# Two edits in a two-layer hybrid diffusion block: gate inputs fetched back in five transfers, and 32 instead of 64 streamed columns in the RWKV doubling levels

## The reference: what is computed

```python
def rwkv_scan(s0, r, w, k, v, kk, a, reverse, emit):
    ...
        sa = jnp.einsum('bhvk,bhk->bhv', s, kk_t)
        s = (s * w_t[:, :, None, :] - sa[..., None] * (kk_t * a_t)[:, :, None, :]
             + v_t[..., None] * k_t[:, :, None, :])
...
def merge_branches(h, ys, w_branch, w_gate, b_gate, w_o):
    gates = jax.nn.sigmoid(h @ w_gate + b_gate)
    acc = gates[..., :D_MODEL] * (ys[0] @ w_branch[0])
    for i in range(1, N_BRANCH):
        acc = acc + gates[..., i * D_MODEL:(i + 1) * D_MODEL] * (ys[i] @ w_branch[i])
    return acc @ w_o
```

## Time and profile before

| | |
|---|---|
| median of 3 runs | 1743.99 us (1742.7 to 1755.26) |
| the profiled execution: its own time | 1740.77 us |
| the profiled execution: span of the trace | 1739.0 us |
| PE busy, weight loads busy | 93%, 76% of the span |
| DVE, ACT, POOL busy | 53%, 45%, 17% |
| mean granted clock of TensorE | 0.973 of 2.4 GHz |
| RWKV passes: forward and reverse of layer 0 | about 347 to 416 and 416 to 491 us |
| RWKV passes: forward and reverse of layer 1 | about 1280 to 1342 and 1342 to 1409 us |

### The profile page before, as it was taken

The page is one execution under the profiler, slowest core; times in us unless marked ns, Lnnn a source line. Parts: engine busy times, 40 slices in busy tenths (PEclk is TensorE's granted clock), DMA queues, the critical chain, the costliest instruction groups (busy, mean ns, idle before and its releaser), DMA issues.

```text
span 1739.0 us, 33048 instructions
## 1 busy us (share of the span) xinstructions
PE 1611.8 (93%) x14136; PEld 1321.1 (76%) x14136; DVE 913.3 (53%) x1438; ACT 783.1 (45%) x1285; POOL 302.3 (17%) x241
## 2 busy tenths in 40 slices
PE   5899999988899998899999998999988889989997
PEld 3678767776666676688888885887776679879997
DVE  3154445476334444555555224565786446567754
ACT  4232355473342233544444223624766453566653
POOL 0041033513010000011112000121452110012201
PEclk8899999999899999999999999999999999989999
DMA  9473345504682222132222534734523284436553
GB/s 324 107 190 98 112 159 176 176 7 148 185 301 73 96 73 73 49 97 97 97 97 62 124 100 148 222 124 134 168 66 124 55 278 155 145 98 194 182 164 116
DMA packets 230496, 234.49 MB, mean 135 GB/s; under 512 B 5904, under 2 KB 217232, under 8 KB 230224
## 3 DMA queue, kind: packets, MB, share of 16 engines
q1 hardware_dynamic: 210720, 190.17, 34.6%
q0 software_dynamic: 15024, 35.92, 7.6%
q10 hardware_dynamic: 4608, 6.29, 1.1%
HBM read 216.63 MB, written 15.73 MB: 134 GB/s over the span
## 4 chain that ended last, share of the span: by engine, by line
PE 67%; DVE 5%; issue 3%; ACT 3%; DMA 0%; POOL 0%; ACTq 0%; DVEq 0%; POOLq 0%
PE ps L1878 16%; PE ps L1879 16%; PE ps L1880 16%; PE ps L2262 5%; PE ps L2120 2%; PE ps L2108 1%; PE ps L1921 1%; PE ps L2159 1%; DVE X L1392 1%; PE ps L2082 1%; PE ps L1901 1%; DVE wlo L1326 1%; PE ps L1902 1%; PE ps L1903 1%; PE ps L1859 1%
## 5 line engine op out<-in xcount | busy, mean ns | idle before, releaser
L899 ACT ACTIVATE whi<-ring 128x1024 fp32r<-128x1024 f32 (+1 forms) x264 | 275.3, 1046 | 550.7 <-PE ps L1880 493.1
L1326 DVE TENSOR_TENSOR wlo<-ring,whi 128x1024 fp32r<-128x1024 f32 (+1 forms) x264 | 326.5, 1242 | 218.5 <-ACT whi L899 217.8
L1878 PE MATMUL ps<-H,whi 128*128 128x512 f32 (+1 forms) x656 | 220.6, 336 | 2.2 <-DVE wlo L1326 2.2
L1880 PE MATMUL ps<-H,wlo 128*128 128x512 f32 (+1 forms) x656 | 220.4, 336 | 0.0
L1879 PE MATMUL ps<-H,whi 128*128 128x512 f32 (+1 forms) x656 | 220.4, 336 | 0.0
L1878 PE MATMUL ps<-HR,whi 128*128 128x512 f32 (+1 forms) x568 | 202.2, 356 | 2.2 <-DVE wlo L1326 1.8
L1880 PE MATMUL ps<-HR,wlo 128*128 128x512 f32 (+1 forms) x568 | 198.3, 349 | 0.0
L1879 PE MATMUL ps<-HR,whi 128*128 128x512 f32 (+1 forms) x568 | 198.1, 349 | 0.0
L1878 PEld LDWEIGHTS ps<-H,whi 128*128 128x128 f32 x656 | 124.5, 190 | 15.6 <-issue 2.8
L1880 PEld LDWEIGHTS ps<-H,wlo 128*128 128x128 f32 x656 | 124.5, 190 | 12.9
L1879 PEld LDWEIGHTS ps<-H,whi 128*128 128x128 f32 x656 | 124.5, 190 | 12.5
(11 more groups left out here) (318 smaller groups left out, 3064.2 us busy)
## 6 DMA issues: line engine op xcount, KB each, us to landing
ring<-in_ffn_up SPq DMA_DIRECT2D x44, 1024.0 KB, 5.1
ring<-in_ada_w SPq DMA_DIRECT2D x40, 1024.0 KB, 5.6
ring<-in_w_gate SPq DMA_DIRECT2D x32, 1024.0 KB, 6.1
ring<-in_w_in SPq DMA_DIRECT2D x24, 1024.0 KB, 7.2
ring<-in_ffn_down SPq DMA_DIRECT2D x32, 512.0 KB, 4.0
ada<-in_ada_w SPq DMA_DIRECT2D x8, 1024.0 KB, 11.9
WB<-in_w_branch POOLq DMA_DIRECT2D x8, 1024.0 KB, 7.5
ring<-in_w_o SPq DMA_DIRECT2D x8, 1024.0 KB, 5.2
```

Source lines behind the costliest of these rows:

```text
L899: act.activation(whi[half_slot(m)][:, 0:kn, :], ring[:, SLOT[raw] % RING, 0:kn, P * half:P * half + P], ACT.Copy).then_inc(hi_done, 1)
L1326: dve.tensor_tensor(wlo[half_slot(m)][:, 0:kn, :], ring[:, SLOT[raw] % RING, 0:kn, P * half:P * half + P], whi[half_slot(m)][:, 0:kn, :].b ...
L1878: pe.matmul(o[:, c0:c1], hi[:, i, :], part(0, k), start=(k == 0), stop=False)
L1880: last = pe.matmul(o[:, c0:c1], lo[:, i, :], part(0, k), start=False, stop=(k == kn - 1))
```

## The change

**Gate inputs.** A helper `hidden_back(part, k0, kn)` fetches `kn` of the 8 row blocks of one part. POOL issues part 1 whole, behind `receptance(1)` and ahead of `to_chunk_end(1)`, that is in the forward chunk loop. Part 0 stays at the old place and comes in four pieces of two row blocks, each issued only when everything before it has landed (`h_back` counts five transfers, and PE waits for all five).

**Levels.** The masks `m2` to `m32` are stored with their 32 non-zero columns alone. `sx` streams only the even blocks of TN's columns, `XS` holds 32 columns of each block, `sy` streams those 32, and TN is updated in its even blocks alone. The number of instructions of each engine but POOL stays the same; POOL issues six transfers more over both layers.

```diff
@@ constants @@
     for z in LEVELS:
-        put(f"m{z}", ((s // z) % 2 == 1) & (t // z == s // z - 1))
+        even = t[:, (t[0] // z) % 2 == 0]
+        put(f"m{z}", ((s // z) % 2 == 1) & (even // z == s // z - 1))
...
-        XS = at("XS", 88, [2, 2, NB, CH])
+        XS = at("XS", 88, [2, 2, NB, CH2])
...
+        def even_blocks(v, z):
+            if len(v.shape) == 2:
+                return v.rearrange("p (g two n) -> p g two n", two=2, n=z)[:, :, 0, :]
+            return v.rearrange("p b y (g two n) -> p b y g two n", two=2, n=z)[:, :, :, :, 0, :]
@@ POOL @@
+                def hidden_back(part, k0, kn):
+                    src = hsave[part, P * k0:P * (k0 + kn), c0:T].rearrange("(k p) t -> p k t", p=P)
+                    pool.dma_start(HG[:, part, k0:k0 + kn, c0:T], src).then_inc(h_back[l], 16)
...
                 receptance(1)
+                pool.wait_ge(h_saved[l], 32)
+                hidden_back(1, 0, KT)
                 to_chunk_end(1)
                 bonus(1)
-                pool.wait_ge(shift_done, 7 * (2 * l + 1) + 7)
                 pool.wait_ge(mm_done, done_at(("tok", l, 1, "k", 1)))
                 pool.wait_ge(bonus_done, 4 * l + 4)
                 pool.wait_ge(lg_done, l + 1)
-                pool.wait_ge(h_saved[l], 32)
-                for part in range(2):
-                    pool.dma_start(HG[:, part, :, c0:T], hsave[part, :, c0:T].rearrange("(k p) t -> p k t", p=P))\
-                        .then_inc(h_back[l], 16)
+                for n in range(HG_PIECES):
+                    pool.wait_ge(h_back[l], 16 * (n + 1))
+                    hidden_back(0, HG_K * n, HG_K)
@@ DVE @@
-                            s = blocks(filled(dve, ("sx", l, d, z, p)))
-                            dve.tensor_tensor(XS[:, p, :, :, :], s, square_mask(f"m{z}"), ALU.mult)\
+                            s = filled(dve, ("sx", l, d, z, p))[:, :, 0:NB * CH2].rearrange("p x (b n) -> p x b n", b=NB)
+                            dve.tensor_tensor(XS[:, p, :, :, :], s, half_mask(f"m{z}"), ALU.mult)\
...
-                            s = blocks(filled(dve, ("sy", l, d, z, p)))
-                            t = TN[:, p, :, :, :].rearrange("p b y n -> p y b n")
+                            s = filled(dve, ("sy", l, d, z, p))[:, :, 0:NB * CH2].rearrange("p y (b g n) -> p b y g n", b=NB, n=z)
+                            t = even_blocks(TN[:, p, :, :, :], z)
@@ PE @@
-                                last = pe.matmul(o[side(y), x, CH * b:CH * b + CH], LM1[side(x), 2 * p + y, b, 0:CH],
-                                                 TN[side(x), p, b, y, :], start=True, stop=True)
+                                last = pe.matmul(o[side(y), x, CH2 * b:CH2 * b + CH2].rearrange("k (g n) -> k g n", n=z),
+                                                 LM1[side(x), 2 * p + y, b, 0:CH], even_blocks(TN[side(x), p, b, y, :], z),
+                                                 start=True, stop=True)
...
-                                last = pe.matmul(o[side(x), y, CH * b:CH * b + CH], TT[side(y), p, b, x, :],
+                                last = pe.matmul(o[side(x), y, CH2 * b:CH2 * b + CH2], TT[side(y), p, b, x, :],
                                                  XS[side(y), p, x, b, :], start=True, stop=True)
...
-                pe.wait_ge(h_back[l], 32)
+                pe.wait_ge(h_back[l], 16 * (1 + HG_PIECES))
```

More of the change, by code:

```diff
@@ L73 @@
 NVEC = _at
+CH2 = CH // 2
+HG_K = 2
+HG_PIECES = KT // HG_K
 CONST_COLS = [("ones", P), ("fold", 2), ("ident", P), ("heads", P), ("swap", P), ("lm", 2 * CH), ("m1", CH),
-              ("m2", CH), ("m4", CH), ("m8", CH), ("m16", CH), ("m32", CH), ("eye", CH), ("cos", LAT), ("sin", LAT),
+              ("m2", CH2), ("m4", CH2), ("m8", CH2), ("m16", CH2), ("m32", CH2), ("eye", CH), ("cos", LAT), ("sin", LAT),
               ("reset", T), ("window", GRID_W)]
@@ L1633, in masked, with half_mask @@
                                           ALU.mult).then_inc(frees((name, l, d, p)), 1)
+                    def half_mask(name):
+                        return K(name, CH2).unsqueeze(1).unsqueeze(1).to_broadcast([P, 2, NB, CH2])
                     def square_mask(name):
@@ L1662, in _ @@
                         for p in range(2):
-                            s = blocks(filled(dve, ("sy", l, d, z, p)))
-                            t = TN[:, p, :, :, :].rearrange("p b y n -> p y b n")
+                            s = filled(dve, ("sy", l, d, z, p))[:, :, 0:NB * CH2]                                .rearrange("p y (b g n) -> p b y g n", b=NB, n=z)
+                            t = even_blocks(TN[:, p, :, :, :], z)
                             if n:
```

## The result

| | median | ratio to before, 95% interval |
|---|---|---|
| changed kernel, 20 runs | 1738.88 us (1729.43 to 1751.35) | 0.9939 [0.9918, 0.9959] |
| before, beside it, 20 runs | 1749.66 us (1741.98 to 1759.26) | |
| changed kernel once more, 8 runs | 1737.52 us | 0.9922 [0.9892, 0.9952] |

The change makes the kernel 0.6% to 0.8% faster, about 11 us. That lies within 1%, as forecast. The forecast time was 1736.7 us, and both medians are within 2.2 us of it. The effect was undersized all the same: 7.3 us were forecast, and the first interval reaches from 7 to 14.

The account below looks back on a forecast made before the run. PE's chain of waits (67%) was taken as the bound. -5.4 - 6.4 - 1.0 + 5.0 + 0.5 = -7.3 us on 1740.8 gave 1733.5; plus 3.2 for the median, 1736.7 us, range 1721 to 1748.

Parts of the forecast that it names:

- Term 1: Matmuls of the levels: halving the moving columns of 2560 matmuls saves 0, with 16.4 us as the upper end.
- the stream was the limit: Rival for the level matmuls: halved columns save 16.4 us, giving 1720.3 us; chance 0.13.
- Term 2: DVE in the levels: one shorter TN update counts per level, 20 x 0.27 = 5.4 us saved (0 to 10.8).
- TN updates bring nothing: Rival for DVE in the levels: shorter TN updates save nothing, giving 1742.1 us; chance 0.10.
- Term 3: Reverse pass, part 0 in pieces: fewer PE stops and clock losses save 6.4 us in layer 0, 1.0 in layer 1.
- the stops have nothing to do with `HG`: Rival for the reverse pass's PE stops: the transfer changes bring 0, giving 1738.6 us; chance 0.15.
- Term 4: Part 1 issued in the forward loop: delayed PE instructions cost 3.5 us in layer 0 and 1.5 in layer 1.
- the second rival: Part 1's flight behind the forward loop costs 22.6 us, more than the pieces give: 1754.3 us; chance 0.12.
- Term 5: Start of the reverse loop: the last piece shares the engines with modulation weights, costing 0.5 us (0 to 1.4).

Follow-up runs that it names:

- 64 streamed columns: The whole change, but `sx` and `sy` stream their 32 columns twice, so 64 as before: 1734.3 us, ratio 0.9927 to before.
- the levels alone: The kernel before with only the 32-column levels; gate inputs return in two whole transfers at the old place: 1743.39 us, ratio 0.996.
- the transfers alone: The kernel before with only the five gate-input transfers changed; levels work on 64 columns as before: 1742.08 us, ratio 0.9962.
- the extra flight: The kernel before plus one unused 2 MB transfer (1 MB in layer 1) in each layer's forward levels: 1753.75 us, ratio 1.0036.
- part 1 at its old place: The whole change, but part 1 is issued whole behind the reverse pass's first three levels, part 0's pieces behind it: 1742.65 us, ratio 0.9971.
- the eight pieces: The whole change, but part 1 also comes in four pieces, all behind the reverse pass's bonus: 1734.01 us, ratio 0.9913; once more 1734.87 us, 0.9897.
- both kernels that stream twice: The whole change with its 32 columns streamed twice (1734.3 us, 0.9927), and the same with both parts in eight pieces (1734.42 us, 0.993), against before.

## Why the prediction held, step by step

**Term 1 (matmuls: 0) was right.** 64 columns instead of 32 change a group by 0.02 to 0.03 us, some 1 us over all groups. The rival "the stream was the limit" is dead: it needed 0.4 us for a group.

**Term 2 (DVE: −5.4) was right in size, and denied something that happens.** The operation is 0.27 us shorter as forecast, and so is the wait ahead of `sx`: 0.40 us became 0.14 in the levels where it is short, and 1.06 became 0.82 where it is longer. What I denied was that the second TN update counts. In `sx` the second half of the 64 matmuls reads the half of TN that the second update writes. The earlier trace rows already show it: the second update ends at 439.01 + 1.29 = 440.30 us, and half of the group that starts at 439.80 would be through at 440.27. In the trace of before the 33rd matmul starts 0.12 us after the 32nd in 12 of the 13 groups that no stop breaks; the others follow each other by 0.015. In after 11 of 16 groups have no such hole, and their starts span 0.92 us instead of 1.07. The same holds with 64 streamed columns (0.94), so it is DVE's doing. By this estimate up to 11 x 0.15 = 1.7 us come on top, 7.1 in all. No run tells 7.1 from 5.4: the levels alone gave 7 us by their runs (3 to 11), and the levels of their trace are 1.3, 1.9, 1.6 and 0.9 us shorter, 5.6 together. A fall of the clock inside the forward levels takes a little back (below). The rival "TN updates bring nothing" is dead.

**Term 3 (pieces: −6.4 and −1.0) was right in layer 0 and too small in layer 1.** The reverse levels of layer 0 took 42.5 us before, 40.5 with the levels alone, and 34.5 to 35.3 in the four traces with part 1 early, part 0 in pieces and the short levels: 5.6 us from the transfers. With the transfers alone they took 36.1, which is 6.4 below before. In layer 1 the same comparisons give 38.1 to a mean of 34.8 (32.4 to 36.1), and 39.0 to 35.2: 3.3 to 3.8 us, not 1.0. I had counted one stop; from the levels to the loop the trace of before has five above 0.5 us, of 0.64, 0.60, 0.64, 1.54 and 0.95, and the trace of after two, of 0.61 and 0.67. My price of a piece was off as well, 6.1 us against 4.0: the packets of a 2 MB part flow for 8.1 us (438.8 to 446.9), where I had derived 5.5 from a rate, so the fixed part was smaller than I took it for. The rival "the stops have nothing to do with `HG`" is dead: the transfers alone bring 0.38%, and the extra flight lengthens stops.

The stops are waits for instruction packets; the kept traces settle that. In the products, levels and read-outs of all 13 traces, 46 stops of 1 us or more are ended by "issue", leaving out 15 at a level's `sx`, where DVE's update of TN can end the wait too. 45 of the 46 end 1.2 to 1.6 us behind the landing of a 16 KB packet of queue q8; of all moments in these stretches 8% lie so. The stop of 4.01 us ended at 421.33, its packet having landed at 419.91. That packet started at 418.96, 0.4 us after the last packet of part 1. The Trainium skill (Runtime: NRT & Kernel Launch, Instruction fetch mechanics) calls the crossing of a 16 KB boundary "mostly hidden"; in these levels, with a large transfer running, it isn't. The stops stand at the same points of PE's list in every kernel, whenever they come. The last 18 matmuls of one job wait 1.90 us before, 3.04 with the levels alone, 3.90 with part 1 at its old place, 0.61 in after; the last 16 of the first products wait 1.27 us before, and 4.01 and 3.21 in the two traces of the change, where they began 1.5 us ahead of part 1's landing and just at it. A flight sets how long such a point costs, but it isn't the only cause: stops of 1.3 to 2.2 us stand also in read-outs where nothing of `h` flies. That size counts is shown at the first of these jobs, in the levels of layer 0: under a whole part it waits 1.90, 3.04, 3.90 and 1.71 us (the last in the kernel with the extra flight), and in the nine traces with pieces there 1.16 at most. Why a packet is late under a flight stays open.

**Term 4 (part 1 in the loop: +3.5 and +1.5) was about right in sum, with nearly all of it in layer 0.** There the stretch to the first level grew from 7.2 to between 10.8 and 12.5 us in the four traces, and the read-out ahead of it from 5.2 to 6.6 in three of them, 5.9 us on average. In layer 1 the two took 8.6 us before and 9.2 on average. The trace of the transfers alone, where part 1 had landed ahead of the products, shows only 0.4 us in layer 0; with it the average of both layers is 5.4. So the price depends on where PE is when the part flies. The stops of 2.49 and 4.01 us are what the second rival named, and the two flights stayed well short of its point of decision (12.3 us). With part 1 whole at its old place the ratio was no better (0.9971).

**Term 5 (+0.5) is nothing.** The last piece was issued at 455.4 us, no "issue" stop follows in the levels, and the reverse loop took 15.6 us (18.4 before).

**Sum.** −7 (levels alone) − 5.6 − 3.5 + 5.9 + 0.7 = −9.5 us, against −10.8 measured (−7 to −14) and −7.3 forecast. The term that was most too small is the one for layer 1 in term 3. That the forecast's time came within 2.2 us is partly luck: it started from the median of three runs, 1744.0 us, which was 5.7 us below that of the 20 runs beside the change, and its effect was 3.5 us too small; the two errors nearly cancel. The expectations for the transfers alone and for part 1 at its old place were my clearest misses. In the second I took the flight behind the loop for dearer than one in the levels; the stop was as long (3.90 us) in the levels.

## What to carry to other kernels

Where PE runs many small matmuls and stops for no reason that a profile shows, look for a large software-queue transfer in flight at that time, and for an instruction packet that landed just before PE went on. Try pieces issued one behind the other before looking for a quieter place: in the levels of layer 0 the same job waited 1.71 to 3.90 us under whole parts and 1.16 at most under pieces, while moving a whole part only moved the stop (4.01 us behind the loop, 3.90 in the levels). Halving the moving columns of 64-column blocks brought about 1 us on PE; the rest came from the shorter vector operations behind it, and both updates of a level counted.

## What the runs showed of the chip that was not expected

- A 512 KB piece from DRAM lands 4.0 us behind its issue, a 2 MB part 10.2 us alone and 13.2 us beside two 1 MB weight transfers.
- Stops are not fixed: under the same two flights they were 1.90 and 3.66 us before, and 3.04 and 0.79 with the levels alone.
- A spell at 1.2 GHz can come or not in the same kernel. The forward loop of layer 0 had 10.2 us of it in the second trace of the change and in the second of the eight pieces, and none in the first of each; it cost 3 us.
- The granted clock in the forward levels of layer 0 (355 to 372 us) was 0.90 in all eight traces with 32 streamed columns and 1.00 in all five with 64 (before, the transfers alone, the extra flight, and both kernels that stream twice). Behind it stands a spell of 3.4 us at 1.2 GHz. A group of the transposes in after takes 1.09 us at 356 us and 1.91 at 362:

```profile
356.23 1.09 PE L2126 MATMUL ps<-con,TN 128*128 128x128 f32 x8
...
361.81 1.91 PE L2126 MATMUL ps<-con,TN 128*128 128x128 f32 x8
```

  0.1 of 17 us is 1.7 us at most. Whether it costs anything in the median stays open: the change with 64 columns (0.9927) and with 32 (0.9939, 0.9922) can't be told apart. Why fewer columns go with it wasn't tried.
- POOL doesn't always issue a transfer at once, though nothing in the program waits. The fourth of four queued transfers of 512 KB came 6.1 us after the third, 0.4 us behind the third's landing. The second whole part of before came 0.3 us behind the landing of the first (447.6 and 447.3 us), so the two never flew together.
